# Shared down weights in a place of their own ahead of the order, and routing counts in their own PSUM bank, in a two-layer mixture-of-experts step

## The reference

```python
def moe(h, router_w, router_b, wg, wu, wd, swg, swu, swd):
    x = h.reshape(-1, D)
    scores = jax.nn.sigmoid((x @ router_w).astype(jnp.float32))
    sel = scores + router_b.astype(jnp.float32)
    ...  # the best 4 of 8 groups, then
    _, eidx = lax.top_k(jnp.where(emask, sel, -jnp.inf), TOP_K)
    w = jnp.take_along_axis(scores, eidx, axis=1)
    w = w / jnp.sum(w, axis=-1, keepdims=True) * ROUTED_SCALE
    routed = routed_experts(x, eidx, w.astype(x.dtype), wg, wu, wd)
    shared = (jax.nn.silu(x @ swg) * (x @ swu)) @ swd
    return (routed + shared).reshape(B, S, D)

# for each expert e and its tokens xb:
hb = jax.nn.silu(xb @ wg[e]) * (xb @ wu[e])
y = (hb @ wd[e]) * w[:, None]
```

## Time and profile before

| what | us |
|---|---|
| median of 3 runs | 1427.31 (1426.31 to 1430.02) |
| the profiled execution's own time | 1427.32 |
| its span, first to last instruction | 1425.5 |
| PE busy | 1379.5 (97%) |
| DVE, ACT, POOL busy | 446.8, 312.6, 48.0 |
| DMA queue of SP, share of 16 engines | 82.1% |

### The profile page before, as it was taken

One profiled execution on the slowest core, in us unless ns is written; L12 is line 12 of the kernel. 1 busy time (PEld: TensorE's weight loads), 2 busy tenths in 40 slices (PEclk: granted clock), 3 DMA queues, 4 the chain that ended last, 5 costly groups with the idle time before them and its releaser, 6 DMA issues.

```text
span 1425.5 us, 20921 instructions
## 1 busy us (share of the span) xinstructions
PE 1379.5 (97%) x8288; PEld 706.5 (50%) x8288; DVE 446.8 (31%) x1287; ACT 312.6 (22%) x746; POOL 48.0 (3%) x86
## 2 busy tenths in 40 slices
PE   7999999999999999999899999999999999999987
PEld 3345656545444445544465456565445445444533
DVE  1136535323221313121345243453221213132123
ACT  2134323111111111111345213421111111111113
POOL 0100302000000000000100010010000000000000
PEclk9999999999999999999999999999999999999998
DMA  9999526999999999999983245289999999999993
GB/s 392 393 372 426 216 118 263 424 425 424 424 427 425 424 426 425 423 426 425 422 329 119 119 160 216 90 344 417 424 428 426 422 425 426 425 426 425 425 421 134
DMA packets 48803, 509.53 MB, mean 357 GB/s; under 512 B 5840, under 2 KB 6240, under 8 KB 9376
## 3 DMA queue, kind: packets, MB, share of 16 engines
q1 hardware_dynamic: 44944, 489.96, 82.1%
q0 software_dynamic: 3760, 18.20, 3.4%
HBM read 499.10 MB, written 11.01 MB: 358 GB/s over the span
## 4 chain that ended last, share of the span: by engine, by line
PE 87%; DMA 5%; DVE 4%; ACT 3%; issue 1%; SPq 0%; DVEq 0%; ACTq 0%
PE bank L2078 26%; PE banks L2128 13%; PE banks L1977 8%; PE banks L459 5%; DMA s_gu_ring<-in_moe_up_dram 4%; PE ybank L2005 3%; PE banks L1136 3%; PE banks L2005 3%; PE bank L2007 3%; PE bank L521 2%; PE ybank L1769 1%; PE banks L1769 1%; DMA s_gu_ring<-in_ada_w_dram 1%; PE banks L714 1%; PE banks L1141 1%; PE banks L688 1%
## 5 line engine op out<-in xcount | busy, mean ns | idle before, releaser
L2078 PE MATMUL bank<-s_gu_ring,s_hbuf 128*32 128x512 f32 (+1 forms) x2688 | 398.2, 598 | 9.6 <-DMA s_gu_ring<-in_moe_up_dram 8.8
L2078 PEld LDWEIGHTS bank<-s_gu_ring,s_hbuf 128*32 128x32 f32 (+1 forms) x2688 | 122.9, 120 | 276.3 <-issue 276.3
L2128 PE MATMUL banks<-s_dn_ring,s_router 128*32 128x512 f32 (+1 forms) x1344 | 204.2, 596 | 0.0
L2245 DVE TENSOR_TENSOR s_ylo<-banks,s_yhi 128x512 fp32r<-128x512 f32 x112 | 77.4, 691 | 324.5 <-ACT s_yhi L2170 324.5
L2170 ACT CAST s_yhi<-banks 128x512 fp32r<-128x512 f32 x112 | 65.6, 586 | 295.5 <-PE banks L2128 295.5
L1977 PEld LDWEIGHTS banks<-s_sel,s_htok 128*128 128x128 f32 x640 | 105.2, 189 | 47.1 <-issue 45.6
L1977 PE MATMUL banks<-s_sel,s_htok 128*128 128x416 f32 (+2 forms) x640 | 125.2, 343 | 1.5 <-DVE s_hbuf L2198 0.9
L2240 DVE SCALAR_TENSOR_TENSOR s_hh<-s_router,s_wsl,bank 128x256 f32<-128x256 f32 x56 | 26.9, 480 | 284.0 <-ACT s_router L2161 284.0
L2128 PEld LDWEIGHTS banks<-s_dn_ring,s_router 128*32 128x32 f32 (+1 forms) x1344 | 55.9, 118 | 117.8 <-issue 117.2
L2161 ACT ACTIVATE s_router<-bank 128x256 f32<-128x256 f32 x56 | 21.5, 384 | 376.2 <-PE bank L2078 376.2
L2198 DVE COPY s_hbuf<-banks 128x416 f32<-128x416 f32 (+2 forms) x60 | 33.9, 565 | 72.7 <-PE banks L1977 72.7
(11 more groups left out here) (461 smaller groups left out, 1458.7 us busy)
## 6 DMA issues: line engine op xcount, KB each, us to landing
s_gu_ring<-in_moe_up_dram SPq DMA_DIRECT2D x126, 2048.0 KB, 19.6
s_dn_ring<-in_moe_wd_dram SPq DMA_DIRECT2D x128, 1024.0 KB, 17.7
s_gu_ring<-in_ada_w_dram SPq DMA_DIRECT2D x24, 2048.0 KB, 13.9
s_gu_ring<-in_win_dram SPq DMA_DIRECT2D x6, 2048.0 KB, 15.7
s_gu_ring<-in_wqkv_dram SPq DMA_DIRECT2D x6, 1024.0 KB, 19.4
s_gu_ring<-in_wo_dram SPq DMA_DIRECT2D x2, 2048.0 KB, 19.9
s_gu_ring<-in_shared_up_dram SPq DMA_DIRECT2D x2, 2048.0 KB, 10.2
s_gu_ring<-in_moe_up_dram SPq DMA_DIRECT2D x4, 1024.0 KB, 26.2
```

Of the source, the lines that this page charges most:

```text
L2078: last = pe.matmul(W0[o:o + n, :], tokens_of(p, k)[:, o - back_by[r]:o - back_by[r] + n], w[:, k, :, :], start=(k == 0), stop=(k == KC - 1))
L2128: last = pe.matmul((W1, W2)[half][o:o + n, :], hTs[:, f, o:o + n], dn_ring[:, DN_PLACE[dn_of[(l, r)][0]], w0:w0 + 512], start=(f == 0), st ...
L2245: dve.tensor_tensor(ylo[:, half, :], (W1, W2)[half], yhi[:, half, :].bitcast(F32), ALU.subtract).then_inc(S["y_low"], 1)
```

## The change

The down ring has four places for experts at first and the fifth for the shared down weights, which are loaded before SP waits for `order`. They are used in passes 4 and 5, not 9 and 10, and the fifth place joins the ring when `shd_used` tells that they are read. `DN_EARLY` falls from five to four, so that down 4 now waits for pass 0's down products. Which place a down load takes is no longer its number modulo five, but the next one that comes free in the order of the passes. The down loads now wait so: 4 and 5 for pass 0, 6 to 8 for pass 1, 9 to 11 for pass 2, 12 and 13 for pass 3, 14 and 15 for pass 4, 16 for `shd_used` in pass 5, 17 and 18 for pass 5 (before: 5 and 6 for pass 0, 7 to 9 for pass 1, 10 to 12 for pass 2, 13 and 14 for pass 3, 15 and 16 for pass 4, 17 and 18 for pass 5). Down 4, 6, 9, 12, 14 and 16 thus wait one step later in the order. Down 19 to 22, and all from 28 on, wait for the same pass as before.

In the routing, the counts go to another bank (`bank[4]`), PE's wait for `tok_hi` moves behind them, and one chunk of `shared_up` instead of three stands between the counts and the two matmuls that make `order`; the other two follow later. The tie constant now tells experts 0 and 1 apart too.

```diff
-NGU, NDN, DN_EARLY = 6, 5, 5
+NGU, NDN, DN_EARLY = 6, 5, 4
...
-SHD_PASS = 9
+SHD_PASS = 4
...
-    ahead = np.where(np.arange(NE) < NFIX, 64.0 * 1024.0, 0.0)
+    ahead = 64.0 * 1024.0 * np.maximum(NFIX - np.arange(NE), 0)
...
-            freed = [None] * NDN
-            shd_at = sum(len(experts) for experts in PASSES[l][:SHD_PASS])
+            places_of, next_pass = [(d, None, None) for d in range(DN_EARLY)], 0
             for r in LOAD_ORDER[l]:
...
-                if i == shd_at:
-                    d = i % NDN
-                    down_in[d].n += 16
-                    shd_of.append((d, down_in[d].n, last_dn[d]))
-                    last_dn[d], freed[d] = (S["shd_used"], l + 1), SHD_PASS + 1
-                d = (i + (i >= shd_at)) % NDN
-                used = None if i < NDN else last_dn[d]
+                if not places_of:
+                    if next_pass == SHD_PASS + 1:
+                        places_of.append((NDN - 1, (S["shd_used"], l + 1), next_pass))
+                    y_done = (S["y_full"], 2 * (l * NP + next_pass + 1))
+                    places_of += [(dn_of[(l, x)][0], y_done, next_pass) for x, _ in PASSES[l][next_pass]]
+                    next_pass += 1
+                d, used, down_free[(l, r)] = places_of.pop(0)
...
                 stored.wait(sp)
+                sp.dma_start(dn_ring[:, DN_PLACE[NDN - 1], :], a["shared_down"][l]).then_inc(down_in[NDN - 1].h, 16)
                 sp.wait_ge(S["order_full"], l + 1)
...
-                    if shd_of[l][2] == (S["y_full"], 2 * (l * NP + p + 1)):
-                        d, _, used = shd_of[l]
-                        sp.wait_ge(*used)
-                        sp.dma_start(dn_ring[:, DN_PLACE[d], :], a["shared_down"][l]).then_inc(down_in[d].h, 16)
...
-                        pe.wait_ge(S["tok_hi"], 6 * l + 6)
                         pe.wait_ge(S["topk_full"], l + 1)
...
-                        pe.matmul(W0[:, 192:256], ones_b, m0, start=True, stop=False)
...
+                        pe.matmul(count[:, 192:256], ones_b, m0, start=True, stop=False)
...
                         last.then_inc(S["cnt_psum"], 1)
+                        pe.wait_ge(S["tok_hi"], 6 * l + 6)
                         pe.matmul(W1[:, 0:64], up, m0, start=True, stop=True)
...
-                        shared_up(0, 0, range(6, KC))
-                        shared_up(0, 1, (0,))
+                        shared_up(0, 0, (6,))
                         pe.wait_ge(S["perm_full"], l + 1)
...
-                        shared_up(0, 1, range(1, KC)).then_inc(S["sh_psum"], 1)
+                        shared_up(0, 0, (7,))
+                        shared_up(0, 1, range(KC)).then_inc(S["sh_psum"], 1)
...
-                        dve.scalar_tensor_tensor(keyr[:, :], W0[:, 192:256], 64.0, cc("keyrow"), ALU.mult, ALU.add)
...
+                        dve.scalar_tensor_tensor(keyr[:, :], count[:, 192:256], 64.0, cc("keyrow"), ALU.mult, ALU.add)
```

More of the change, by code:

```diff
@@ L1581, in decoder_step @@
         excess = sb("excess", [P, 2], I32)
-        last_dn = [None] * NDN
-        shd_of, last_half = [], sem("last_half")
+        last_half = sem("last_half")
         gu_of, dn_of, down_free = {}, {}, {}
         def expert_slots(l):
-            freed = [None] * NDN
-            shd_at = sum(len(experts) for experts in PASSES[l][:SHD_PASS])
+            places_of, next_pass = [(d, None, None) for d in range(DN_EARLY)], 0
             for r in LOAD_ORDER[l]:
@@ L1605, in expert_slots @@
                 last_item[s] = (S["gu_full"], l * NP + pass_of[l][r] + 1)
-                last_dn[d] = (S["y_full"], 2 * (l * NP + pass_of[l][r] + 1))
-                down_free[(l, r)], freed[d] = freed[d], pass_of[l][r]
         def expert_stream(l, dn_ring):
@@ L1685, in moe @@
                 dn_ring = sb("dn_ring", [P, NDN, DNW], c=c)
+                down_in[NDN - 1].n += 16
+                shd_d, shd_n = NDN - 1, down_in[NDN - 1].n
                 expert_slots(l)
-                shd_d, shd_n, _ = shd_of[l]
                 expert_stream(l, dn_ring)
@@ L1729, in _ @@
                             pool.tensor_tensor(lo, tok32[t][0:tn, :], hi.bitcast(F32), ALU.subtract).then_inc(S["tok_lo"], 1)
-                    logit, logit2, R1 = bank[6], bank[4][0:NE, 0:NS], bank[6][:, 256:320]
+                    logit, logit2, R1, count = bank[6], bank[4][0:NE, 0:NS], bank[6][:, 256:320], bank[4]
                     @block.tensor
@@ L1786, in _ @@
                         m0, m1, m2 = mb2[:, 0, 0, :], mb2[:, 1, 0, :], mb2[0:NS, 2, 0, :]
-                        pe.matmul(W0[:, 192:256], ones_b, m0, start=True, stop=False)
-                        pe.matmul(W0[:, 192:256], ones_b, m1, start=False, stop=False)
-                        pe.matmul(W0[:, 192:256], ones_b[0:NS, :], m2, start=False, stop=True)
+                        pe.matmul(count[:, 192:256], ones_b, m0, start=True, stop=False)
+                        pe.matmul(count[:, 192:256], ones_b, m1, start=False, stop=False)
+                        pe.matmul(count[:, 192:256], ones_b[0:NS, :], m2, start=False, stop=True)
                         for t, (t0, tn) in enumerate(TILES):
-                            last = pe.matmul(W0[:, 256:258], mb2[0:tn, t, :, :].rearrange("p u e -> p (u e)"), ones_b[0:tn, 0:2], start=(t == 0), stop=(t == 2))
+                            last = pe.matmul(count[:, 256:258], mb2[0:tn, t, :, :].rearrange("p u e -> p (u e)"), ones_b[0:tn, 0:2], start=(t == 0), stop=(t == 2))
                         last.then_inc(S["cnt_psum"], 1)
+                        pe.wait_ge(S["tok_hi"], 6 * l + 6)
                         pe.matmul(W1[:, 0:64], up, m0, start=True, stop=True)
@@ L1879, in _ @@
                         dve.wait_ge(S["cnt_psum"], 2 * l + 1)
-                        dve.scalar_tensor_tensor(keyr[:, :], W0[:, 192:256], 64.0, cc("keyrow"), ALU.mult, ALU.add)
-                        dve.tensor_copy(cols[:, 2:3], W0[:, 256:257])
-                        step(dve.scalar_tensor_tensor(cols[:, 0:1], W0[:, 256:257], 64.0, cc("keycol"), ALU.mult, ALU.add))
+                        dve.scalar_tensor_tensor(keyr[:, :], count[:, 192:256], 64.0, cc("keyrow"), ALU.mult, ALU.add)
+                        dve.tensor_copy(cols[:, 2:3], count[:, 256:257])
+                        step(dve.scalar_tensor_tensor(cols[:, 0:1], count[:, 256:257], 64.0, cc("keycol"), ALU.mult, ALU.add))
                         step(dve.tensor_scalar(over[:, :], keyr[:, :], cols[:, 0:1], None, ALU.is_gt))
```

## The result

The changed kernel takes 1445.16 us (median of 4 runs, 1438.48 to 1446.58), the kernel before 1427.67 (4 runs): ratio 1.011, 95% interval 1.0093 to 1.0127. It is slower, as forecast, but by 17.5 us and not by 9.4, beyond the range. The profiled execution took 1446.58 us with a span of 1444.8, that is 19.3 more than before.

A forecast was written before the change was run, and what follows sets the result against it. Weight transfers bound the stage's end; PE, 14.7 us late at up 22, lets the queue run dry: stream 7.1 later, minus 2.47 for the shared load. 4.6 + 4.8 = 9.4 us on 1427.32 gives 1436.7; range 1432 to 1440, 8 in 10 1430 to 1441.

The forecast's parts named there:

- shared products: Shared down products leave passes 9 and 10 for 4 and 5, making PE 9.2 us later by pass 6.
- wait in pass 2: No wait ahead of pass 2's down products was put in the sum.
- wait in pass 3: PE waits 4.4 us (3.2 to 5.0) for down 9 ahead of pass 3's down products.
- shared load gone: The shared down load goes ahead of the order, into an empty queue; 2.47 us per layer leave the full stream.
- end of the layer: The transfer stream ends 4.6 us later in layer 0 and 4.8 in layer 1, and stays the bound.
- The order and pass 0: In the routing, `order` comes some 1.3 us earlier per layer; pass 0's start unchanged, 0.6 us gain as bound.
- The head start: Up 5 lands at 256.3, not 260.1; of 3.8 us gained, 3 are lost at up 6 to an empty queue.
- The tie of the stream to PE: Pass 1 issues up 8 at 270.41, landing at 279.4 at the earliest, so PE again sets the stream.
- more waits: Rival, chance 0.06: down 7 lands close to pass 2's down products; another 1.4 to 3 us per layer, 1440 to 1443.
- The slow start: Pass 3's products run slowly at a lower clock behind the wait, costing 1.1 us (0 to 1.4).
- The refill: An up load into an empty or nearly empty queue lands 9.0 us after issue (7.8 to 9.8), at up 6 and up 22.
- the reserve by up 20: Up 20 landed 16.3 us after issue, 9.0 into an empty queue, so 7.3 us of lateness cost nothing.

The follow-up runs named there:

- The run with PE kept busy: The changed kernel with twelve small matmuls of no use ahead of pass 3's wait for down 9: 1439.61 us, ratio 1.0075.
- the pads: Kernel before, useless matmuls ahead of pass 3's down products: 36, 1439.57 us; 17, 1429.9; with shared down products in passes 4 and 5, 1444.34 and 1434.38.
- the long pad: The kernel before with 36 small matmuls of no use ahead of pass 3's down products: 1439.57 us, ratio 1.0076.
- the run with the places alone: The changed kernel with counts and order of chunks as before; four places, shared load and tie constant stay changed: 1444.5 us, 1.0119.
- the run interleaved in passes 2 to 9: The changed kernel, shared products in passes 9 and 10; in passes 2 to 9 SP issues one up load, freed down loads, other up loads: 1432.0 us, 1.0019.

## Why the direction was right and the size wrong

The mechanism was right: waits for down loads, a slow start, shared products that make PE later still, a queue that runs dry in passes 5 to 7, transfers that remain the bound. What failed are sizes in the sum: PE's lateness at up 22 was put at 14.7 us and measured 17.7 in layer 0, with the wait of pass 2 at nothing and the slow products at 1.1, and the refill was put at 9.0 and measured 9.9 and 10.3. Nearly all missed to the slower side. Layer 0, and layer 1 where it differs:

| term | predicted, us | measured, us |
|---|---|---|
| pass 0 | 0 (bound -0.6) | -0.56 |
| wait in pass 2 | 0 | 1.46; 1.31 |
| wait in pass 3 | 4.4 (3.2 to 5.0) | 4.99; 4.17 |
| slow products behind it | 1.1 (0 to 1.4) | 2.55; 2.75 |
| shared products | 9.2 | 9.28 |
| refill: up 22, issue to landing | 9.0 (7.8 to 9.8) | 9.88; 10.30 |
| shared load gone | -2.47 | -2.48 |
| end of the layer | +4.6; +4.8 | +8.87; +9.06 |

The waits are differences of lateness; they exceed the idle times (1.39 and 4.91 in layer 0) by under 0.1 us, as before the down products began while the matmuls ahead of them ended. Layer 0 follows from its rows: -0.56 + 1.46 + 4.99 + 2.55 + 9.28 = 17.7 late at up 22 instead of 14.7, and the refill 0.9 longer: 3.9 us more than the 4.6 forecast makes 8.5; pass 27's slow start added the rest. Between the layers the profiled run lost another 1.3 us.

**The order and pass 0.** `order` came 1.57 us earlier (1.3 forecast). Pass 0 gained 0.56 in layer 0, the bound.

**The head start.** Up 6 landed at 262.5 (264.3 forecast), up 8 at 280.1 (279.4 at the earliest), down 4 at 269.9, with no wait of pass 1. The tie of the stream to PE held. But the step stopped at down 5. Down 6 moved from pass 0's issues (264.48) to pass 1's (281.86), ahead of down 7, which pass 2 needs: with one load more ahead (2.5) and up 8 0.3 later it lands at 294.84 instead of 292.04, and 294.07 is when pass 2's down products began before. The prediction has this only as the first half of the rival "more waits". Its own list of loads gives 279.4 + 2 x 4.95 + 2 x 2.47 = 294.2 for down 7, already behind 294.07, so a small wait belonged in the sum; the rest came from up 8, 0.7 us later than its earliest, and from PE, 0.56 earlier.

**Pass 3.** Down 9 was issued at 298.81 and landed 16.5 later, at 315.3 (314.0 forecast).

**The slow start** missed its bound by most, 2.55 and 2.75 us against 1.4. I priced it by pass 27, where a low stretch lay partly in the wait (granted clock 0.83 on average in the last 1.7 us ahead of its products); from 315 to 322 the granted clock is 0.60 on average, most of it at the lower of the two levels, and the products took 2.56 us longer. The run with PE kept busy puts its worth at some 3.6 of the 17.5 us.

**The refill.** Up 22 took 9.9 and 10.3 us, above the high end. The prediction named the row of 9.8, at a queue that was not quite empty, as up 22's case, and yet took 9.0. Up 6 was issued 0.9 us before the load ahead of it landed and took 7.8; up 8 and up 22, issued 2.5 and 3.2 before, took 10.2 and 9.9: what was left of the load ahead came on top. By the fit on the Trainium skill's page DMA: Bandwidth & Descriptors (section Anatomy of one DMA), which is for transfers issued by GpSimd, 2 MB would take an estimated 6.8 us. No 2 MB load that went into an empty or nearly empty queue here was that short (7.7 to 10.3 after), so the rows decide, and the sum by the page would have been further off.

**What the parts are worth.** The sum charged the shared products' 9.2 us to the change, and set the reserve by up 20. Both hold for the kernel after, but not as a cause. The 9.2 us drain the queue wherever they stand: with five places the pads measure a reserve of 2 to 3 us when they stand in passes 9 and 10, and next to none in 4 and 5. Moving them costs nothing alone (0.9995). Moving them back gains nothing (1.0109): PE then waits a third time (1.6 and 0.7 us), and a place is still missing there. That these two take the reserve is argued; the trace shows only the holes. The pads show the rule from the other side: 3.8 us of lateness in each layer cost 1.0010 (0 to 3 us in all, helped by pass 27's clock) in the one place and 1.0044 (4 to 9 us) in the other. So the loss is the 8.4 us by which PE stays late after passes 2 and 3 in each layer. It comes from the fifth place that passes 0 to 3 lack, by way of SP's order of issue: with the down loads of pass 2 ahead of two up loads, the same four places cost 1.0017.

**What stays open.** What starts the low stretch between the layers (1.3 us after), and what the last combination waited for with the long pad. Whether a sixth place would keep the head start and avoid the waits was not tried.

## What to carry to other kernels

A ring of buffers has its reserve at its shallowest point: take issue to landing of every load behind the delay, look for the shortest, and count the delay against that load, not against a convenient one. The number so found is a bound, not the reserve (4.0 us by up 29, 3.4 by up 35, 2 to 3 measured by the pads), and a time that agrees can hide a gain elsewhere, as pass 27's clock did here: compare the last landing, too. Taking a place out of the ring moves every later load by one, so follow each load to the pass that needs it. An experiment that leaves work out also returns that work's time to the engine, so a pad that adds the suspected delay to the kernel before is the better test.

## What the hardware showed beside this

**A queue that is nearly empty doesn't hide the next load's start.** In a full queue up loads land 4.9 us apart. In the trace after, up 20 was issued 0.55 us before the load ahead of it landed, up 8 2.51 and up 22 3.15 before; they landed 7.5, 7.7 and 6.7 us after that load. An issue 3 us ahead of the queue's end still lost 1.8 us of transfer. In the trace before, up 8 was issued 4.46 us ahead and landed 4.9 us after that load, with no loss; in layer 1 it was 4.12 ahead and landed 5.7 after.

**The low clock doesn't follow from the length of the wait alone.** The 1.39 us in pass 2 left the products at 3.64 us, and so did 2.10 in the run with the places alone and 2.25 in the run interleaved in passes 2 to 9. But 2.17 with the shared products left out gave 5.28, and 2.10 in layer 1 of the run with the down loads ahead in pass 2 gave 5.34. Pass 27 took 8.43 us before behind 3.48 us of wait, but 7.07 behind 3.45 in the run interleaved in passes 2 to 9. And after has a low stretch between the layers, behind an idle time of 0.62 us; before has the same idle time there, and its clock stays at 1.00 (window of after, columns as in rows 1):

```profile
880.40:883.80 3.40, 3.40 (x11) 2.42 (x10) 0.00 (x0) 0.00 (x0) 0.89 (x1) 0.51 0.11 40
```
